# Second expert product: eleven of its 64 pairs of chunks per layer multiplied as two by two blocks with seven products

## What is computed

```python
s1, i1 = lax.top_k(s[..., 0, :], PEER_TOPK); s2, i2 = lax.top_k(s[..., 1, :], PEER_TOPK)
...
u = jnp.take(expert_down, idx, axis=0)
act = jax.nn.gelu(jnp.einsum('btd,bthkd->bthk', xi, u).astype(jnp.float32))
v_sel = jnp.take(expert_up, idx, axis=0)
return jnp.einsum('bthk,bthkd->btd', (g * act).astype(xi.dtype), v_sel)
```

## Time and profile before

| | |
|---|---|
| median of 3 runs | 2083.38 us |
| the profiled execution, its own time | 2080.16 us |
| its span, first to last instruction | 2078.4 us |
| granted TensorE clock, mean | 0.999 |
| second expert product, layer 0 | about 570 to 912 us |
| second expert product, layer 1 | about 1468 to 1810 us |

### The profile page before, as it was taken

One profiled execution on the slowest core, in us unless ns is written; L12 is line 12 of the kernel. 1 busy time (PEld: TensorE's weight loads), 2 busy tenths in 40 slices (PEclk: granted clock), 3 DMA queues, 4 the chain that ended last, 5 costly groups with the idle time before them and its releaser, 6 DMA issues.

```text
span 2078.4 us, 31213 instructions
## 1 busy us (share of the span) xinstructions
PE 2059.3 (99%) x11872; PEld 1767.0 (85%) x11872; DVE 1458.5 (70%) x2611; ACT 1289.7 (62%) x2205; POOL 374.6 (18%) x183
## 2 busy tenths in 40 slices
PE   8999999999999999999999999999999999999998
PEld 8788988888888888887888888888888888888888
DVE  8969988889865555567589788889655555543456
ACT  6665688887654444466656888877544444554674
POOL 2457700000000000012378000000000000045241
PEclk9999999999999999999999999999999999999999
DMA  6455755555566666664457655555666666676444
GB/s 229 153 162 173 231 175 173 164 177 168 171 193 195 192 197 192 194 215 136 125 171 223 192 163 171 164 173 170 187 191 193 193 195 193 205 222 194 131 155 140
DMA packets 108458, 376.25 MB, mean 181 GB/s; under 512 B 12372, under 2 KB 17908, under 8 KB 107412
## 3 DMA queue, kind: packets, MB, share of 16 engines
q1 hardware_dynamic: 107444, 369.00, 57.5%
q0 software_dynamic: 864, 5.24, 1.2%
HBM read 367.87 MB, written 1.08 MB: 178 GB/s over the span
## 4 chain that ended last, share of the span: by engine, by line
PE 95%; DVE 3%; ACT 1%; issue 1%; POOL 0%; DMA 0%; DVEq 0%; SPq 0%; ACTq 0%
PE ps L184 28%; PE ps L178 15%; PE ps L180 15%; PE ps L179 15%; PE ps L185 14%; PE ps L1086 3%; PE ps L1065 1%; DVE arena L791 1%; PE ps L1109 1%; DVE WL L166 0%; DVE arena L788 0%; PE ps L2219 0%; PE ps L2243 0%; PE ps L1112 0%; PE ps L1679 0%
## 5 line engine op out<-in xcount | busy, mean ns | idle before, releaser
L161 ACT ACTIVATE WH<-raw 128x1024 fp32r<-128x1024 f32 x680 | 717.3, 1057 | 458.3 <-PE ps L180 372.1
L184 PE MATMUL ps<-X,WH 128*128 128x512 f32 x2528 | 895.7, 398 | 0.1
L166 DVE TENSOR_TENSOR WL<-raw,WH 128x1024 fp32r<-128x1024 f32 x554 | 680.6, 1230 | 59.8 <-ACT WH L161 59.1
L185 PE MATMUL ps<-X,WL 128*128 128x256 f32 x2528 | 707.0, 280 | 0.0
L171 POOL TENSOR_TENSOR WL<-raw,WH 128x1024 fp32r<-128x1024 f32 x126 | 319.4, 2558 | 1590.3 <-ACT WH L161 1588.2
L184 PEld LDWEIGHTS ps<-X,WH 128*128 128x128 f32 x2528 | 474.0, 187 | 107.7 <-issue 0.6
L185 PEld LDWEIGHTS ps<-X,WL 128*128 128x128 f32 x2528 | 477.3, 189 | 0.1
L178 PE MATMUL ps<-WH,X 128*128 128x512 f32 (+1 forms) x960 | 378.2, 394 | 1.6 <-DVE X L390 1.0
L180 PE MATMUL ps<-WH,X 128*128 128x512 f32 (+1 forms) x960 | 373.8, 389 | 0.0
L179 PE MATMUL ps<-WL,X 128*128 128x512 f32 (+1 forms) x960 | 373.6, 389 | 0.0
L178 PEld LDWEIGHTS ps<-WH,X 128*128 128x128 f32 x960 | 180.6, 188 | 41.8 <-issue 2.1
(11 more groups left out here) (318 smaller groups left out, 2097.5 us busy)
## 6 DMA issues: line engine op xcount, KB each, us to landing
raw<-in_l_down_dram SPq DMA_DIRECT2D x256, 512.0 KB, 3.6
raw<-in_l_up_dram SPq DMA_DIRECT2D x256, 512.0 KB, 4.2
raw<-in_l_wq_dram SPq DMA_DIRECT2D x32, 512.0 KB, 3.6
raw<-in_w_qk_dram SPq DMA_DIRECT2D x24, 512.0 KB, 3.7
raw<-in_w_gates_dram SPq DMA_DIRECT2D x24, 512.0 KB, 3.6
raw<-in_l_nat_dram SPq DMA_DIRECT2D x16, 512.0 KB, 3.5
raw<-in_l_wout_dram SPq DMA_DIRECT2D x16, 512.0 KB, 3.4
raw<-in_l_win_dram SPq DMA_DIRECT2D x16, 512.0 KB, 4.1
```

Source lines behind the costliest of these rows:

```text
L161: a.activation(WH[:, i % NW, :], raw[:, i % NW, :], ACT.Copy).then_inc(w_high, 1)
L166: v.tensor_tensor(WL[:, i % NW, :], raw[:, i % NW, :], WH[:, i % NW, :], ALU.subtract).then_inc(w_low_v, 1)
L184: t.matmul(PS[:, bank, :], w[0], X2[:, k, :, :].rearrange("p w t -> p (w t)"), start=first, stop=False)
L185: return t.matmul(PS[:, bank, 0:256], w[1], X2[:, k, 0, :], start=False, stop=last)
```

## The change

For the pairs p = 16, 20, ..., 56 (`SEVEN`: eleven in each layer) the pair's four token-by-expert blocks (two token halves, two chunks) and four expert-by-column blocks (two chunks, two column halves) are multiplied as a two by two block product with seven block products instead of eight. Each still is a `three`.

- PE: `seven_own` does three products on the pair's own blocks, one while chunk 2p is its turn (three matmuls) and two for chunk 2p+1 (six). `seven_sums` does the four products that need summed weight blocks later, behind chunk 2p+4 (twelve). Banks 0 to 3 collect four partial results, beside banks 4 to 7.
- VectorE: `seven_rows` and `seven_weights` form four sums of row blocks and four of weight blocks; `seven_rows_low` and `seven_weights_low` make their low parts. At the end of the loop `seven_add`, in four steps at c = 120 to 123, combines banks 0 to 3 and adds them to X.
- ScalarE: `seven_scalar` makes the high parts of the sums, one of 512 and two of 1024 columns, and once per layer copies banks 0 and 1 out.
- The first chunk of such a pair is split over 512 of its 1024 columns only (`width`), and the load that reuses the slots of such a pair also waits until the weight sums have been read.
- Some semaphores of other stages are merged into one another (`eps_up` with `lb_in`, and so on), without a change in order.

```diff
+        with nc.sbuf_tensor("split_t", [128, 2, 4, 512], F32R) as SPLIT_T:
...
-        x_in, cst_in, pv_in, eps_up = [sem(f"x_in{i}") for i in range(4)], sem("cst_in"), sem("pv_in"), sem("eps_up")
+        x_in, cst_in, pv_in, eps_lb_up = [sem(f"x_in{i}") for i in range(4)], sem("cst_in"), sem("pv_in"), sem("eps_bounds_up")
...
+        SEVEN = tuple(range(16, 57, 4))
+        IN_SEVEN = {base + 144 + 2 * p + j: (len(SEVEN) * l + m, j)
+                    for l, base in enumerate((P0, P1)) for m, p in enumerate(SEVEN) for j in range(2)}
+        seven_v, seven_a, seven_done = (sem("seven_" + n) for n in ("sums_low", "high", "products"))
+        def width(i):
+            return 512 if IN_SEVEN.get(i, (0, 1))[1] == 0 else SLOT
...
+            if i - NW in IN_SEVEN:
+                m, j = IN_SEVEN[i - NW]
+                s.wait_ge(seven_v, 9 * m + 6 + j)
...
-            a.activation(WH[:, i % NW, :], raw[:, i % NW, :], ACT.Copy).then_inc(w_high, 1)
+            w = width(i)
+            a.activation(WH[:, i % NW, 0:w], raw[:, i % NW, 0:w], ACT.Copy).then_inc(w_high, 1)
...
-                v.tensor_tensor(WL[:, i % NW, :], raw[:, i % NW, :], WH[:, i % NW, :], ALU.subtract).then_inc(w_low_v, 1)
+                w = width(i)
+                v.tensor_tensor(WL[:, i % NW, 0:w], raw[:, i % NW, 0:w], WH[:, i % NW, 0:w],
+                                ALU.subtract).then_inc(w_low_v, 1)
...
+        SUM_T, SUM_S = ar(4096, 4, 512), ar(6144, 5, 128)
+        HIGH_T, LOW_T = (SPLIT_T[:, w, :, :] for w in range(2))
+        HIGH_S, LOW_S = (X2[:, 6 + w, :, :].rearrange("p w t -> p (w t)") for w in range(2))
         def parts_g(p):
+            if p in SEVEN:
+                return [X2[:, w, :, :].rearrange("p w t -> p (w t)") for w in range(2)]
...
+            def seven_own(p, j):
+                m, i = SEVEN.index(p), up + 2 * p + j
+                gh, gl = parts_g(p)
+                hw, lw = WH[:, i % NW, :], WL[:, i % NW, :]
+                if j == 0:
+                    if m == 0:
+                        t.wait_ge(act_gated, N_HEAD * l + N_HEAD)
+                    a_ = [w[:, 0:128] for w in (gh, gl)]
+                    e = three(t, PS[:, 0, :], a_, [w[:, 0:512] for w in (hw, lw)], m == 0, m == len(SEVEN) - 1)
+                else:
+                    a_ = [w[:, 256:384] for w in (gh, gl)]
+                    three(t, PS[:, 4, :], a_, [w[:, 0:512] for w in (hw, lw)], False, False)
+                    t.wait_ge(seven_v, 9 * (len(SEVEN) * l + m) + 4)
+                    a_ = [w[:, 0:128] for w in (HIGH_S, LOW_S)]
+                    e = three(t, PS[:, 5, :], a_, [w[:, 512:1024] for w in (hw, lw)], False, False)
+                e.then_inc(w_used, 1)
+            def seven_sums(p):
+                m = SEVEN.index(p)
+                gh, gl = parts_g(p)
+                t.wait_ge(seven_v, 9 * (len(SEVEN) * l + m) + 8)
+                for n, (bank, part) in enumerate(((1, 1), (2, 3), (3, 2), (6, None))):
+                    if n == 2:
+                        t.wait_ge(seven_v, 9 * (len(SEVEN) * l + m) + 9)
+                    a_ = ([w[:, 384:512] for w in (gh, gl)] if part is None
+                          else [w[:, part * 128:part * 128 + 128] for w in (HIGH_S, LOW_S)])
+                    e = three(t, PS[:, bank, :], a_, [w[:, n, :] for w in (HIGH_T, LOW_T)],
+                              n < 3 and m == 0, n < 3 and m == len(SEVEN) - 1)
+                e.then_inc(seven_done, 1)
...
             for c in range(124):
                 up_ready(c)
-                for tt in range(2):
-                    up_products(c, tt)
+                if c // 2 in SEVEN:
+                    seven_own(c // 2, c % 2)
+                else:
+                    for tt in range(2):
+                        up_products(c, tt)
+                if c % 2 == 0 and c // 2 - 2 in SEVEN:
+                    seven_sums(c // 2 - 2)
...
+            if p in SEVEN:
+                a.wait_ge(seven_done, len(SEVEN) * l + SEVEN.index(p))
...
+        def seven_scalar(a, l, c):
+            for m, p in enumerate(SEVEN):
+                u, r = len(SEVEN) * l + m, c - 2 * p
+                if r == -3:
+                    a.wait_ge(seven_done, u)
+                    a.wait_ge(seven_v, 9 * u + 3)
+                    a.activation(HIGH_S, SUM_S[:, 0:4, :].rearrange("p a b -> p (a b)"), ACT.Copy).then_inc(seven_a, 1)
+                if r in (-1, 0):
+                    a.wait_ge(seven_done, u)
+                    a.wait_ge(seven_v, 9 * u + (7 if r == 0 else 5))
+                    w = slice(2 * r + 2, 2 * r + 4) if r == 0 else slice(0, 2)
+                    a.activation(HIGH_T[:, w, :], SUM_T[:, w, :], ACT.Copy).then_inc(seven_a, 1)
+            if c == 2 * SEVEN[-1] + 7:
+                a.wait_ge(seven_done, len(SEVEN) * (l + 1))
+                a.activation(SUM_T[:, 0:2, :], PS[:, 0:2, :], ACT.Copy).then_inc(seven_a, 1)
...
                 high(a, up + c + 3)
                 if c % 2 == 0:
                     split_g_scalar(a, l, c // 2 + 1)
+                seven_scalar(a, l, c)
...
+        def seven_rows(v, l, p):
+            u, o = len(SEVEN) * l + SEVEN.index(p), 6144
+            g = G[:, 2 * p:2 * p + 2, :]
+            def two_places(at, to):
+                return bass.AP(AR, at, [[32768, 128], [to - at, 2], [1, 128]])
+            if u:
+                v.wait_ge(seven_v, 9 * u)
+            v.tensor_tensor(SUM_S[:, 3:5, :], g[:, :, 0:128], g[:, :, 128:256], ALU.subtract).then_inc(seven_v, 1)
+            v.wait_ge(seven_v, 9 * u + 1)
+            v.tensor_tensor(SUM_S[:, 0:2, :], two_places(o + 512, 512 * p + 128), two_places(o + 384, 512 * p + 384),
+                            ALU.add).then_inc(seven_v, 1)
+            v.tensor_tensor(SUM_S[:, 2, :], g[:, 1, 128:256], SUM_S[:, 3, :], ALU.subtract).then_inc(seven_v, 1)
+        def seven_rows_low(v, l, p):
+            u = len(SEVEN) * l + SEVEN.index(p)
+            v.wait_ge(seven_a, 3 * u + l + 1)
+            v.tensor_tensor(LOW_S, SUM_S[:, 0:4, :].rearrange("p a b -> p (a b)"), HIGH_S, ALU.subtract).then_inc(seven_v, 1)
+        def seven_weights(v, l, p, step):
+            u, i = len(SEVEN) * l + SEVEN.index(p), bases(l)[2] + 2 * p
+            first, second = raw[:, i % NW, :], raw[:, i % NW + 1, :]
+            if step == 0:
+                v.wait_ge(raw_in[(i + 1) % NW], 16 * ((i + 1) // NW + 1))
+                v.tensor_tensor(SUM_T[:, 0:2, :], raw[:, i % NW:i % NW + 2, 512:1024],
+                                first.rearrange("p (a b) -> p a b", a=2), ALU.subtract).then_inc(seven_v, 1)
+            else:
+                v.wait_ge(seven_v, 9 * u + 5)
+                v.tensor_tensor(SUM_T[:, 2, :], SUM_T[:, 1, :], first[:, 0:512], ALU.add).then_inc(seven_v, 1)
+                v.wait_ge(seven_v, 9 * u + 6)
+                v.tensor_tensor(SUM_T[:, 3, :], second[:, 0:512], SUM_T[:, 2, :], ALU.subtract).then_inc(seven_v, 1)
+        def seven_weights_low(v, l, p, step):
+            u, w = len(SEVEN) * l + SEVEN.index(p), slice(2 * step, 2 * step + 2)
+            v.wait_ge(seven_a, 3 * u + l + step + 2)
+            v.tensor_tensor(LOW_T[:, w, :], SUM_T[:, w, :], HIGH_T[:, w, :], ALU.subtract).then_inc(seven_v, 1)
+        def seven_add(v, l, step):
+            if step == 0:
+                v.wait_ge(seven_a, (3 * len(SEVEN) + 1) * (l + 1))
+                v.tensor_tensor(SUM_T[:, 2, :], PS[:, 3, :], SUM_T[:, 0, :], ALU.add).then_inc(vec.sem, vec.up())
+            if step == 1:
+                v.wait_ge(vec.sem, vec.n)
+                v.tensor_tensor(PS[:, 1:3, :], PS[:, 1:3, :], SUM_T[:, 2, :].unsqueeze(1).to_broadcast([128, 2, 512]),
+                                ALU.add).then_inc(vec.sem, vec.up())
+            if step == 2:
+                v.wait_ge(vec.sem, vec.n)
+                v.tensor_tensor(PS[:, 3, :], PS[:, 2, :], SUM_T[:, 1, :], ALU.add).then_inc(vec.sem, vec.up())
+            if step == 3:
+                v.wait_ge(vec.sem, vec.n)
+                xv = X[:, :, :].rearrange("p t n -> p (t n)")
+                v.tensor_tensor(xv, xv, PS[:, 0:4, :].rearrange("p a n -> p (a n)"), ALU.add).then_inc(vec.sem, vec.up())
+        def seven_vector(v, l, c):
+            for p in SEVEN:
+                r = c - 2 * p
+                if r == -4:
+                    seven_rows(v, l, p)
+                if r == -3:
+                    seven_rows_low(v, l, p)
+                if r in (-2, -1):
+                    seven_weights(v, l, p, r + 2)
+                if r in (1, 3):
+                    seven_weights_low(v, l, p, r // 2)
+            if 0 <= c - 2 * SEVEN[-1] - 8 < 4:
+                seven_add(v, l, c - 2 * SEVEN[-1] - 8)
...
+                if c // 2 + 1 in SEVEN:
+                    seven_vector(v, l, c)
                 if c % 2 == 0:
                     split_g_vector(v, l, c // 2 + 1)
+                if c // 2 + 1 not in SEVEN:
+                    seven_vector(v, l, c)
```

(34 more changed lines are left out.)

1 line of the change is left out of this document (added).

## The result

| | before | changed |
|---|---|---|
| median of 20 runs each | 2081.45 us (2079.22 to 2084.15) | 2085.77 us (2082.57 to 2089.23) |
| ratio, with its 95% interval | | 1.0022 (1.0015 to 1.0028) |
| span of the profiled execution | 2078.4 us | 2082.9 us |
| second expert product on PE, layer 0 | 345.25 us | 347.27 us |
| the same, layer 1 | 345.24 us | 347.25 us |

PE does 66 matmuls fewer and the kernel is 0.22% slower, 4.3 us by the medians. The kernel before was run more often for this table: the three runs that the prediction started from, median 2083.38, are among its 20, whose median is 1.9 us lower.

The account below looks back on a forecast made before the run. PE's back-to-back matmuls were taken to bound the second expert product. Saved matmuls -14.96, new waits +15.0 and loop ends +1.4 made +1.4 us on the 2083.38 median: 2084.8 us, range 2078 to 2095.

Parts of the forecast that it names:

- the side that was given 0.25: Whole kernel: outcome slower than the 0.2% (4.2 us) no-change band, chance 0.25.
- the saved matmuls: PE, second expert product: 66 matmuls fewer over 22 pairs at 0.2267 us each, 14.96 us gained if PE never waited.
- The chain to the next pair: ScalarE's high part, split, then VectorE's low part: operand ready at 2.56 us, PE at 2.04; wait 0.68 us per pair with restart.
- The price of the restart: PE after a wait for VectorE: 0.06 us to the first matmul, second at 0.33 instead of 0.227, 0.16 us together.
- the sum of +1.4: Whole kernel: -14.96 saved, +15.0 waits, +1.4 at the loop ends, giving +1.4 us.
- The end of the loop: VectorE's closing additions make chunk 127 0.68 us late in each layer, 1.4 us in all, bounds 0 and 3.
- Covered work: Added sums and parts, VectorE some 150 us busier and ScalarE some 50, lie beside PE and cost no time.
- The 1.15 us that VectorE was to have spare: VectorE before the next pair's activation low part: free at +0.72 us, needed at +1.87, so 1.15 us spare.
- the 1.77 us of the rival: VectorE-late rival: the two dependent weight sums take 1.77 us each, 1.0 us more per pair, 2107 us, chance 0.08.
- the wait is not paid: Faster rival at PE's wait for the next pair: a chain link is shorter or PE held elsewhere, 2069.8 us, chance 0.14.
- The swinging clock: Rival on PE: small gaps halve the clock for one chunk after each wait, 60 us more, 2145 us, chance 0.03.
- Late loads: Rival before pair p+2: four-slot ring's loads late beyond 6.1 us landing; at 6.5 us landing 2094 us, chance 0.12.

Follow-up runs that it names:

- split first: Changed kernel with ScalarE's split of the next pair's activations moved ahead of the high part that waits for PE, at changed pairs: 2068.75 us, ratio 0.9942.
- waits swapped: Changed kernel with PE's two waits before an even chunk reordered, activations first, then the chunk's weights: 2081.78 us in one run.
- eight products: Changed kernel with all added sums, low and high parts kept, but PE multiplying every pair with the old 24 matmuls: 2083.09 us, ratio 1.0011.

## Why the prediction was right, and where its sum was short

**The total: nearer than its parts.** 2085.77 us is 1.0 us above the 2084.8 forecast, and part of that is luck. The change was forecast at +1.4 us and is +4.3; that is 2.9 us more, of which 1.9 do not show in the time, because the kernel before came out 1.9 us lower in 20 runs than in the first three. The forecast's own line for "no change" was 0.2%, and 0.22% lies just beyond it, on the side that was given 0.25. The range, 2078 to 2095, held the time.

**What bounds it, and the saved matmuls: right.** 66 matmuls went, and where nothing waits each brings 0.2267 us: with the split first, a product is 345.25 - 338.50 = 6.75 us shorter, that is 11 x 0.68 = 7.48 less the 0.7 at the end of the loop.

**The chain to the next pair: right, to 0.01 us.** 2.57 us from the pair's start to the end of the low part, forecast as 2.56 from places where nobody waited for it; 22 waits of 0.5 us, ended by the operation named. Moving one instruction in ScalarE's list removes them all; taking VectorE's sums away removes none.

**The price of the restart: too small, the term that was mis-sized.** I took 0.16 us from the first two matmuls of the earlier trace rows. In the changed kernel a period of four pairs, from one restart at 660.10 to the next at 681.98, is 21.88 us; its 93 matmuls at 0.2267 make 21.08, so a wait costs 0.80 us. Of it 0.52 is the gap until the low part's end, as forecast, and 0.28 the restart: 0.14 until the first matmul, 0.08 that the second is late beyond the usual step, and some 0.05 in those that follow. 22 x (0.80 - 0.68) = 2.6 us is what the sum of +1.4 lacked: 4.0 us, which is what the two products show. The bounds I gave for the wait, 0.52 to 0.84, held it. Of the 0.12 that were missing, 0.06 stand before the second matmul: it begins 0.45 us after the low part, 0.39 in the earlier trace rows, and with PE's two waits swapped 0.40. The rest lies in the matmuls behind, which I didn't read; the trace before has it too, where behind the earlier trace rows thirteen steps from 1012.48 to 1015.47 take 2.99 us and not 2.95. Only 0.5 us of each wait is listed as idle. The other 0.3 us lie under rows that count as busy, 6.6 us in 22 waits, which is why PE's busy time fell by 8.3 us and not by 15.

**The end of the loop: right.** 0.68 us per layer forecast, 0.68 read above and 0.72 and 0.74 with the eight products, by the low parts of chunks 126 and 127 behind the 2.28 us addition.

**Covered work: right.** VectorE went up by 125 us (150 forecast), ScalarE by 47 (50), and the kernel that does all of it with the old products is 1.6 us slower than before, the end of the loop and little else. The 1.15 us that VectorE was to have spare ahead of the low part are there, as its idle time of 1.15 us before 659.27. They rest on the second dependent sum of weights ending at -0.41, which the prediction puts down without a working: two starts 0.61 apart behind -1.75 give -0.53. In the changed kernel it ends at 656.98, which is -0.41; the two sums last 0.69 us each and start 0.72 apart, so neither took the 1.77 us of the rival.

**The rivals.** That the wait is not paid happened only once ScalarE's list was changed. The granted clock stayed at 1.00 in every stretch of both products, with 22 gaps of PE of 0.9 us from matmul to matmul, one in 21.88 us within a layer. The swinging clock of which the Trainium skill ("TensorE: Matmul & The Clock Gate", "A second HAM failure mode: psum-queue depth-cycling") tells did not come. That page of the Trainium skill speaks of frequent gaps, and one in 21.88 us is no test of it. Late loads came nearer than I had them. The landings in 655 to 900 us of the changed kernel, and ScalarE's waits for loads in 600 to 910:

```profile
DMA to landing us min/median/max: 3.4/4.3/6.4
...
ACT WH L177 <- DMA raw<-in_l_up_dram: 4.4, 5, 2.2
```

6.4 us at the longest, where the kernel before had 5.3 and my limit was 6.1; and ScalarE waited for loads five times, where in the kernel before it waited for none. But the limit was for the load of chunk 2p+5, and with the loads counted in the order of their issue its 22 loads took 5.4 us at the longest. The load of 6.4 us brought chunk 124, behind the last changed pair. ScalarE's longest wait, 2.2 us, was for a load of 6.3 us that brought chunk 112; its low part was done at 870.17, and PE began that chunk at 876.16, 6 us later. PE's 22 gaps are all 0.90 us from matmul to matmul, so no late load made one of them longer.

## What to carry to other kernels

When work is taken from the engine that sets the time at one place of a loop, ask first what the next step there waits for: a chain that was hidden behind 5.4 us of matmuls was not hidden behind 2.0, and its length could be read from the old trace where nobody waited for it. If one link of that chain stands in its engine's list behind an instruction that waits for the saved engine itself, move the link ahead of it: here that one move is the difference between 0.2% lost and 0.6% won.

## What was not expected

Restarting PE after a wait cost 0.28 us, and only half of it stands before the first matmul; the rest is a late second matmul and a few behind it that stand 0.23 to 0.24 us apart. The weight loads (PEld) of the first two matmuls of pair 17 show where the second one's delay comes from:

```profile
660.07 0.19 PEld L196 LDWEIGHTS ps<-WH,X 128*128 128x128 f32 x1 [0.90 <-issue]
...
660.18 0.19 PEld L197 LDWEIGHTS ps<-WL,X 128*128 128x128 f32 x1
```

The second matmul, at 660.41, stands 0.23 us behind its weight load, as one does without a wait (0.22 in the median); but the load itself starts only 0.08 us after the first matmul, where without a wait it starts with it. So the second matmul is late because its weight load is. This is read from the rows, and no run tried it.

Where PE has two waits ahead of a matmul, the order in which they are written matters. The end of the loop with the waits swapped, where chunk 126 is released by the second of them:

```profile
911.17 2.36 DVE L183 TENSOR_TENSOR WL<-raw,WH 128x1024 fp32r<-128x1024 f32 x2
...
912.54 0.47 PE L196 MATMUL ps<-WH,GH 128*128 128x512 f32 x1
```

Released by the second, PE began 0.14 us after VectorE's operation (pairs of the changed kernel) or 0.15 us (chunk 126 with the waits swapped: its low part ends at 911.17 + 1.22 = 912.39, the matmul starts at 912.54). Released by the first, or by an only wait, it began after 0.06 us (chunks 126 and 127 of the changed kernel, the pairs with the waits swapped). To the second matmul the difference is smaller, 0.45 us against 0.40. So the wait that is met last belongs first, for some 0.06 us each time. Why it is so was not tried.
